# Sixth product of the MLP's first stage in the joined form, and two additions of the last chunks placed earlier on VectorE

## What is computed

```python
SEQ, D_MODEL, MLP_HIDDEN, DEPTH = 512, 1024, 4096, 2

def _rms_norm(x, g):
    y = x * lax.rsqrt(jnp.mean(x * x, axis=-1, keepdims=True) + RMS_EPS)
    return y * g

def _squared_relu_mlp(h, w1, w2):
    return jnp.square(jax.nn.relu(h @ w1)) @ w2

for layer in range(DEPTH):
    h = _rms_norm(x, norm_mix_g[layer])
    x = x + mixer(h)                       # attention in layer 0, retention in layer 1
    h = _rms_norm(x, norm_ffn_g[layer])
    x = x + _squared_relu_mlp(h, ffn_w_in[layer], ffn_w_out[layer])
return _rms_norm(x, final_g)
```

## Time and profile before

| | |
|---|---|
| Time, median of 3 runs | 1245.82 us (1245.33 to 1245.84) |
| The profiled execution's own time | 1246.04 us |
| Its span, first to last instruction | 1244.2 us |
| PE busy | 1233.8 us (99%) |
| DVE, ACT, POOL busy | 983.8, 779.0, 297.0 us |
| Granted TensorE clock | 0.999 of full speed |

### The profile page before, as it was taken

One profiled execution on the slowest core, in us unless ns is written; L12 is line 12 of the kernel. 1 busy time (PEld: TensorE's weight loads), 2 busy tenths in 40 slices (PEclk: granted clock), 3 DMA queues, 4 the chain that ended last, 5 costly groups with the idle time before them and its releaser, 6 DMA issues.

```text
span 1244.2 us, 18372 instructions
## 1 busy us (share of the span) xinstructions
PE 1233.8 (99%) x6870; PEld 1064.4 (86%) x6870; DVE 983.8 (79%) x1280; ACT 779.0 (63%) x1088; POOL 297.0 (24%) x330
## 2 busy tenths in 40 slices
PE   9999999999999999999999999999999999999997
PEld 6788888898888988889898889898889888898886
DVE  6588647598889798898666797567898988979888
ACT  6688755477575675765656645556677747466474
POOL 2343653111211112101131212231231122111220
PEclk9999999999999999999999999999999999999999
DMA  7367567778988989874968597969589898889983
GB/s 246 98 135 165 134 152 193 206 204 195 226 212 229 228 184 231 216 224 111 226 138 188 137 232 170 220 153 233 99 224 245 209 202 218 228 221 210 226 202 107
DMA packets 147976, 238.89 MB, mean 192 GB/s; under 512 B 51104, under 2 KB 72872, under 8 KB 147888
## 3 DMA queue, kind: packets, MB, share of 16 engines
q0 software_dynamic: 32352, 102.79, 44.0%
q1 hardware_dynamic: 115232, 134.60, 34.1%
q10 hardware_dynamic: 304, 0.33, 0.1%
HBM read 127.57 MB, written 2.11 MB: 104 GB/s over the span
## 4 chain that ended last, share of the span: by engine, by line
PE 87%; DVE 6%; issue 2%; ACT 2%; DMA 1%; SPq 0%; POOLq 0%; POOL 0%; ACTq 0%; DVEq 0%
PE banks L1072 19%; PE banks L1452 11%; PE banks L1030 11%; PE banks L998 6%; PE banks L1520 6%; PE banks L1241 6%; PE banks L1041 6%; PE banks L1401 5%; PE banks L1181 4%; PE banks L1035 3%; PE banks L1466 2%; PE banks L1343 2%; PE banks L1208 2%; DVE w L2356 2%; PE banks L1415 1%
## 5 line engine op out<-in xcount | busy, mean ns | idle before, releaser
L2356 DVE TENSOR_TENSOR w<-raw_tiles,w 128x1024 fp32r<-128x1024 f32 x312 | 371.7, 1220 | 33.8 <-ACT w L1662 33.8
L1662 ACT ACTIVATE w<-raw_tiles 128x1024 fp32r<-128x1024 f32 x312 | 316.3, 1052 | 129.6 <-PE banks L1072 60.8
L1072 PE MATMUL banks<-w,arena_q 128*128 128x512 f32 x1332 | 305.2, 390 | 0.7 <-DVE x L2696 0.7
L3378 POOL DMA_DIRECT2D raw_tiles<-raw_tiles x176 | 152.3, 905 | 629.9 <-DVE w L2356 358.1
L1072 PEld LDWEIGHTS banks<-w,arena_q 128*128 128x128 f32 x1332 | 248.7, 188 | 53.9 <-DVE x L2696 2.0
L1452 PE MATMUL banks<-w,h_ops 128*128 128x512 f32 x672 | 154.0, 390 | 0.0
L1452 PEld LDWEIGHTS banks<-w,h_ops 128*128 128x128 f32 x672 | 125.6, 188 | 25.7
L1030 PE MATMUL banks<-h_ops,w 128*128 128x512 f32 x576 | 144.1, 392 | 0.0
L1030 PEld LDWEIGHTS banks<-h_ops,w 128*128 128x128 f32 x576 | 104.0, 189 | 18.8
L1041 PEld LDWEIGHTS banks<-h_ops,w 128*128 128x128 f32 x576 | 78.6, 190 | 5.6
L998 PE MATMUL banks<-h_ops,w 128*128 128x256 f32 x672 | 82.0, 283 | 0.0
(11 more groups left out here) (253 smaller groups left out, 1886.3 us busy)
## 6 DMA issues: line engine op xcount, KB each, us to landing
raw_tiles<-raw_tiles POOLq DMA_DIRECT2D x176, 512.0 KB, 5.6
raw_tiles<-in_ffn_w_in SPq DMA_DIRECT2D x64, 512.0 KB, 6.2
raw_tiles<-in_ffn_w_out SPq DMA_DIRECT2D x64, 512.0 KB, 6.1
raw_tiles<-in_odd_w_in SPq DMA_DIRECT2D x32, 512.0 KB, 5.3
raw_tiles<-in_even_w_in SPq DMA_DIRECT2D x48, 256.0 KB, 3.5
raw_tiles<-in_odd_w_in SPq DMA_DIRECT2D x32, 256.0 KB, 5.5
raw_tiles<-in_odd_w_out SPq DMA_DIRECT2D x16, 512.0 KB, 6.0
raw_tiles<-raw_tiles POOLq DMA_DIRECT2D x20, 256.0 KB, 4.1
```

The source lines that it names most:

```text
L1072: mm = pe.matmul(bank[first + t][:, :], a_ring[a_slot(g, i)][:, a, k, P * t:P * t + P], w_slots[use_slot(use)][:, b, k, :], start=(starts ...
L1662: nc.scalar.activation(w_flat(use_slot(use), 0, half), raws[tile][:, 1024 * half:1024 * half + 1024], ACT.Copy).then_inc(m_hi, 1)
L2356: nc.vector.tensor_tensor(w_flat(use_slot(use), 1, half), raws[use_tile(key)][:, 1024 * half:1024 * half + 1024], w_flat(use_slot(use), 0, ...
L3378: pool.dma_start(raws[dst][:, part], raws[src][:, part], accum_op=ALU.add).then_inc(t_made[value][half], 16)
```

## The change

The set `WIDE` goes: all seven products of `wide_first_stage` take the joined form. Since product 5 now also writes the cross half of its bank, `wide_x_cross(g, HIGH, b)` waits for product 5 instead of product 4 and is placed behind it. In the last chunks the additions are ordered (4, 0) before (3, 0) and (3, 1). In chunk 3 the addition (5, 0) is placed before `variance(2, 0)`, and the split `use_lo(("qk", 0, 0), 0)` behind it. Chunk 7's list has the first of the two moves only. Orders are now lists of (product, half), and the ACT wait of `square_sum` for t = 0 follows the new order.

```diff
+ADD_ORDER = [(i, t) for i in (0, 1, 4, 5, 2, 3, 6) for t in range(2)]
+LAST_ORDER = [(0, 0), (0, 1), (1, 0), (1, 1), (2, 0), (2, 1), (4, 0), (3, 0), (3, 1), (4, 1), (5, 0), (5, 1), (6, 0), (6, 1)]
 FIRST_X, FIRST_Z, FIRST_Y = 2, 0, 4
 WIDE_X, WIDE_Z = (2, 6), (4, 0)
-WIDE = (0, 1, 2, 3, 4, 6)
...
                             if c == 0 and k % 2 == 0:
                                 pe.wait_ge(m_lo, 2 * use + k // 2 + 1)
-                            if i in WIDE:
-                                pe.matmul(dst.rearrange("p (q n) -> p q n", q=2), w_slots[use_slot(use)][:, 0, k, c:c + P],
-                                          h_ops[:, H_BLOCK[op], :, k, :],
-                                          start=(i < 3 and k == 0), stop=(k == 3), skip_group_check=True)
-                                continue
-                            for n, (p, q) in enumerate(PASSES):
-                                mm = pe.matmul(dst[:, 0:256], w_slots[use_slot(use)][:, p, k, c:c + P],
-                                               h_ops[:, H_BLOCK[op], q, k, :],
-                                               start=False, stop=(k == 3 and n == 2), skip_group_check=True)
...
+                            pe.matmul(dst.rearrange("p (q n) -> p q n", q=2), w_slots[use_slot(use)][:, 0, k, c:c + P],
+                                      h_ops[:, H_BLOCK[op], :, k, :],
+                                      start=(i < 3 and k == 0), stop=(k == 3), skip_group_check=True)
+                    for dst, c in columns:
+                        for k in range(4):
+                            mm = pe.matmul(dst[:, 0:256], w_slots[use_slot(use)][:, 1, k, c:c + P],
+                                           h_ops[:, H_BLOCK[op], 0, k, :],
+                                           start=False, stop=(k == 3), skip_group_check=True)
                     mm.then_inc(p_done, 1)
...
                 elif t < 2:
-                    act.wait_ge(p_added, added(CHUNKS * (norm // 2) - 1, 4, t))
+                    act.wait_ge(p_added, added(CHUNKS * (norm // 2) - 1, 3 if t == 0 else 4, t))
...
                 dve.wait_ge(cross_added[2 if low else 1], wide_count(g) + b + 1)
-                dve.wait_ge(p_done, use_done(first_use(g, 4), b))
+                dve.wait_ge(p_done, use_done(first_use(g, 4 if low else 5), b))
...
-                if add_before(g, i):
-                    dve.wait_ge(p_added, added(*add_before(g, i), t))
+                if add_before(g, i, t):
+                    dve.wait_ge(p_added, added(*add_before(g, i, t)))
...
                     for b in range(2):
                         wide_x_cross(g, LOW, b)
-                        wide_x_cross(g, HIGH, b)
                         wide_x(g, LOW, b)
                     w_lo(stage, 6, 1)
                     w_lo(stage + 1, 0, 0)
+                    wide_x_cross(g, HIGH, 0)
                     wide_x(g, HIGH, 0)
+                    wide_x_cross(g, HIGH, 1)
                     wide_x(g, HIGH, 1)
...
                 w_lo_both(stage + 1, 5)
+                add_product(g, 4, 0)
                 if last:
                     add_product(g, 3, 0)
                     add_product(g, 3, 1)
-                add_product(g, 4, 0)
                 operand_lo(g, 6)
                 add_product(g, 4, 1)
                 w_lo_both(stage + 1, 6)
...
                 norm = 2 if g < CHUNKS else 4
                 if norm == 2:
-                    use_lo(("qk", 0, 0), 0)
+                    add_product(g, 5, 0)
                 variance(norm, 0)
...
-                add_product(g, 5, 0)
+                use_lo(("qk", 0, 0), 0)
                 normed(norm, 0)
```

More of the change, by code:

```diff
@@ L235, in products_done, with add_before @@
     return use_done(second_use(g, i), t)
+ADD_ORDER = [(i, t) for i in (0, 1, 4, 5, 2, 3, 6) for t in range(2)]
+LAST_ORDER = [(0, 0), (0, 1), (1, 0), (1, 1), (2, 0), (2, 1), (4, 0), (3, 0), (3, 1), (4, 1), (5, 0), (5, 1), (6, 0), (6, 1)]
 def add_order(g):
-    return (0, 1, 2, 3, 4, 5, 6) if g % CHUNKS == CHUNKS - 1 else (0, 1, 4, 5, 2, 3, 6)
+    return LAST_ORDER if g % CHUNKS == CHUNKS - 1 else ADD_ORDER
 def added(g, i, t=1):
-    return 14 * g + 2 * add_order(g).index(i) + t + 1
-ADDS = [(g, i) for g in range(2 * CHUNKS) for i in add_order(g)]
-def add_before(g, i):
-    same = [key for key in ADDS[:ADDS.index((g, i))] if PRODUCTS[key[1]][3] == PRODUCTS[i][3]]
+    return 14 * g + add_order(g).index((i, t)) + 1
+ADDS = [(g, i, t) for g in range(2 * CHUNKS) for i, t in add_order(g)]
+def add_before(g, i, t):
+    same = [key for key in ADDS[:ADDS.index((g, i, t))] if PRODUCTS[key[1]][3] == PRODUCTS[i][3] and key[2] == t]
     return same[-1] if same else None
@@ L711, in trunk @@
         z_added = sem("z_added")
-        low_cross = sem("low_cross")
-        high_cross = sem("high_cross")
+        x_crossed = sem("x_crossed")
         last_copied = sem("last_copied")
@@ L1028, in wide_first_stage @@
                                 pe.wait_ge(m_lo, 2 * use + k // 2 + 1)
-                            if i in WIDE:
-                                pe.matmul(dst.rearrange("p (q n) -> p q n", q=2), w_slots[use_slot(use)][:, 0, k, c:c + P],
-                                          h_ops[:, H_BLOCK[op], :, k, :],
-                                          start=(i < 3 and k == 0), stop=(k == 3), skip_group_check=True)
-                                continue
-                            for n, (p, q) in enumerate(PASSES):
-                                mm = pe.matmul(dst[:, 0:256], w_slots[use_slot(use)][:, p, k, c:c + P],
-                                               h_ops[:, H_BLOCK[op], q, k, :],
-                                               start=False, stop=(k == 3 and n == 2), skip_group_check=True)
-                    if i in WIDE:
-                        for dst, c in columns:
-                            for k in range(4):
-                                mm = pe.matmul(dst[:, 0:256], w_slots[use_slot(use)][:, 1, k, c:c + P],
-                                               h_ops[:, H_BLOCK[op], 0, k, :],
-                                               start=False, stop=(k == 3), skip_group_check=True)
+                            pe.matmul(dst.rearrange("p (q n) -> p q n", q=2), w_slots[use_slot(use)][:, 0, k, c:c + P],
[6 more added lines that the diff above has]
+                                           start=False, stop=(k == 3), skip_group_check=True)
                     mm.then_inc(p_done, 1)
@@ L2647, in wide_x_cross @@
                 dve.wait_ge(cross_added[2 if low else 1], wide_count(g) + b + 1)
-                dve.wait_ge(p_done, use_done(first_use(g, 4), b))
-                nc.vector.tensor_tensor(v, v, wide_part(4, b, HIGH), ALU.subtract).then_inc(low_cross if low else high_cross, 1)
+                dve.wait_ge(p_done, use_done(first_use(g, 4 if low else 5), b))
+                nc.vector.tensor_tensor(v, v, wide_part(4, b, HIGH), ALU.subtract).then_inc(x_crossed, 1)
             def wide_x(g, tokens, b):
@@ L2654, in wide_x @@
                 v = hidden_part(1, b, tokens)
-                dve.wait_ge(low_cross if low else high_cross, wide_count(g) + b + 1)
+                dve.wait_ge(x_crossed, 2 * wide_count(g) + (0 if low else 2) + b + 1)
                 dve.wait_ge(p_done, use_done(first_use(g, 4 if low else 5), b))
```

## The result

The changed kernel takes 1252.46 us (median of 6 runs, 1251.24 to 1256.38), the kernel before 1245.45 beside it (6 runs, 1244.95 to 1245.84): a ratio of 1.0062 [1.0052, 1.0072], 7.0 us slower. The forecast was 1244.8, the range 1243.6 to 1246.2. The prediction was wrong: the time lies outside the range, on the side that had a chance of 0.03. The profiled execution took 1256.38 us, the highest of the six, with a span of 1254.6. It shows the loss larger than the median does; what follows takes up what differs from run to run.

A forecast was written before the change was run, and what follows sets the result against it. PE was taken to bound the kernel, DVE in chunks 3 and 7. Savings of 1.04 and 0.09 less 0.13 give 1.00 us, profiled 1246.04 to 1245.04; less 0.22 to the median, forecast 1244.8, range 1243.6 to 1246.2.

The forecast's parts named there:

- Part 1: Product 5 joined in six chunks: 32 instead of 48 matmuls, 0.175 us saved a chunk, 1.04 us in all.
- the 0.17 that the prediction made its test: Chunks 1, 2, 5 and 6 each get 0.17 us shorter, or the prediction is wrong.
- Part 2: Cross subtractions behind product 5 on DVE: no reader late, cost taken as zero, range 0 to 0.1 us a chunk.
- the check on the second stage's first operand: Operand's low part ready 5.47 us after product 6's start, when PE's weight load wants it: no slack, no wait.
- rival C: Second stage's first operand late by more than 0.1 us; at 0.35 us a chunk, +0.4, 1246.2; chance 0.08.
- The check on product 6: HIGH subtraction ends 5.28 us after product 5's start, PE's weight load wants 5.48: 0.15 us left, no wait.
- Part 3: Chunk 3's reordered additions: 0.6 + 0.35 us of PE waits removed, only 0.09 us gained, bounds 0 and 0.95.
- Part 4: Chunk 7, (4, 0) first: PE's gain falls off the path, 0.13 us lost; bounds −0.2 (a gain) and +0.13.
- A: Last chunks' waits come back in full, as PE sets the end there: 2.6 us less, 1243.2; chance 0.07.
- D: A matmul costs by its columns alone, so the joined form saves nothing: 1245.9; chance 0.05.
- E: The change doesn't do what it says on PE in the six chunks; given no chance.
- B: Retention layer's DMA landing swallows the first layer's gain of chunks 1 to 3: 1245.4; chance 0.10.

The follow-up runs named there:

- e3: The whole change, with DVE's split of the second stage's first weights, second half, placed ahead of operand sum S1; 1245.21 us, ratio 0.9997 to the kernel before.
- e7: Joined product 5 with the weight split ahead of S1, the last chunks' lists as in the kernel before; 1244.61 us, ratio 0.9989 to that kernel.
- e12: Joined product 5, weight split ahead of S1, last chunks as in the kernel before: the same kernel as e7, run again; 1244.86 us, ratio 0.9994.
- e2: The kernel before with only the moved additions of the last chunks, product 5 in the separate form; 1246.28 us, ratio 1.0004.
- e10: As e7, and in the last chunks only addition (4, 0) ahead of the two additions 3; 1245.09 us, ratio 0.9996 to the kernel before.
- e4: The kernel before with one small POOL operation ahead of the weight sum T1's second half, in six chunks; 1245.96 us, ratio 1.0002.
- e5: The kernel before with four small POOL operations (128x3) ahead of the weight sum T1's second half, in six chunks; 1259.7 us, ratio 1.0111.
- e9: The kernel before with two small POOL operations (128x3) ahead of the weight sum T1's second half, in six chunks; 1251.82 us, ratio 1.005.
- e6: The changed kernel, with POOL's third sum, first half, waiting until T1's second half has landed; 1251.61 us, ratio 1.0042 to the kernel before.

## Why the prediction was wrong, point by point

**Part 1, the joined form: about right in size.** A half takes 2.79 to 2.80. The stretches from chunk 1 to 3 and from 5 to 6 are 0.10 to 0.15 us shorter where nothing else is late (e3, e7, e12), not quite the 0.17 that the prediction made its test; PE's second stage reads 38.16 us there instead of 38.11. The stretch from 6 to 7 is not shorter, by chunk 7's own wait. With the split put right the mean is 1.0 us below the kernel before, against 1.04 reckoned. The formula of the Trainium skill ("TensorE: Matmul & The Clock Gate", section "Back-to-back issue gap"), which the page gives for an isolated matmul, made this an estimated 0.24. The runs are nearer to the rows.

**Part 2: here the prediction failed.** In chunk 1 its times on DVE were right to 0.01 us, and in five chunks so was the check on the second stage's first operand: the stage starts 5.58 to 5.59 after product 6, with no wait where rival C looked for one. The check on product 6 held in chunk 1, but in chunk 7 its 0.15 us of slack was not enough: DVE began 0.37 later there, for a reason that the trace doesn't settle, and 0.22 us was lost. The failing step is the sentence "DVE is not itself in the way: the S1 sum and one split behind it end by 4.0", with "nothing is passed on" behind it. The reckoning had just moved everything from the second subtraction on by 0.73 us, and this split was part of it. It asks whether DVE is free for the next operand, and not who waits for the split itself. On POOL's queue the split's end releases the sum T1; the sum's landing releases ACT, and ACT was there at that very moment. The rows were in the trace of before: the split at 358.25, POOL waiting for it at 360.01, ACT at 364.63 and DVE waiting 0.89 for ACT at 365.72. The term that was set at zero is 0.72 us in each of six chunks, 4.3 us, plus about 1.7 to 2.2 us each time the landing takes its longer time. With the joined form's −1.0 and the last chunks' +0.6 this gives 3.9 us with no long landing. With three of them (1.67, 2.2 and 1.9 more), as in the profiled execution, it gives about 9.7; 10.4 were measured there, and 0.6 to 0.8 of them lie between the retention layer's start and chunk 5. The median's 7.0 lies between, so some 3 us of it rest on long landings, whose cause is open.

**Part 3, chunk 3: wrong by 0.6 us.** "POOL's `rstd` is done by then" was taken with the 0.6 us that it needs beside a bank addition. Beside the moved split it takes 1.47. The turn comes 0.48 us later relative to the second stage (e2: 35.61 against 35.13), not 0.09 earlier. The dependent pair (0.13) was right: e10 shows 0.12.

**Part 4, chunk 7: right.** From its second stage to the end takes 46.25 us in e2 against 46.18, and 46.08 in e10 against 45.96 in e12. That is about 0.1 each time (the spans are given to a tenth), for 0.13 reckoned, and PE's gain does fall off the path.

**The rivals.** A, D and E are out: removing PE's waits in the last chunks shortened nothing, the form gives about what the rows said, and the lists did what was written. C named the side and a wait of the second stage, but its mechanism, the first operand, did not happen. B happened in part: in the changed kernel the retention layer and chunk 4 took 0.62 us more although the joined form saves 0.17 in it, by a sum that landed after 7.5 us instead of 6.0 at 690.92. But in e7 this stretch keeps all of the gain (485.02 for 485.63), and with the same kernel in e12 it does not (486.82). So it is a landing that varies from execution to execution, and not one that holds the stretch at a fixed length.

**The range** was too narrow because its widening terms were all bounds on costs that I had listed. No term stood for a queue that I had not followed, in an edit that shifts what stands behind it on DVE by 0.7 us in six chunks. Its inner bound of 1243.9 leaves out part 4's (0.2 gained for 0.13 lost); with it the bound is 1243.6, which changes nothing in the outcome.

## What to carry to other kernels

When an edit moves instructions in an in-order list by some tenths, go through every instruction behind the edit, not only those whose consumers come to mind, and look up who waits for each one on each engine's queue, the one that issues DMAs above all. A DMA whose landing coincides with the engine that comes for it has no slack; the profile of before shows no wait there, and only the difference between the landing and the need tells. If a list must be longer, put the instruction that releases a transfer first, and the arithmetic that nobody waits for behind it: here one exchange of two neighbours, in six chunks, was worth 7 us.

## What the runs showed of the hardware

- GpSimd's `rstd` (128x1) took 0.55 to 0.56 us beside a VectorE operation that reads PSUM, and 1.47 us beside a 128x1024 VectorE split with both inputs in SBUF. Other small GpSimd operations took 0.19 us (e4, and the first of each row in e5 and e9). Where a row's next one started just behind such a split it took 1.17 to 1.21 us and ended with it (e9: 360.13 to 361.34, the split 360.07 to 361.30), so the 1.37 us of e9's two are one short and one long.
- An accumulating transfer of one weight half (512 KB) between SBUF tiles took 4.54 to 4.59 us from issue to landing, or 6.2 to 6.7, in the same kernel and place. It took 4.5 or 6.3 with nothing else in its queue (e6). In the retention layer the like one took 6.0, 6.8 or 7.5. In the seven long ones behind the split, fifteen of sixteen completions came by 4.6 us and the last one alone 1.65 to 2.2 us later. The cause is open.
